# A transformer trunk's first FFN: the Winograd scheme's first step replaced by a plain one, and the modulation weights summed on TensorE

## The reference

```python
mod = silu(c) @ w_ada + b_ada                       # c (1, 1024), w_ada (1024, 9*1024)
(sh1, sc1, gt1, sh2, sc2, gt2, sh3, sc3, gt3) = split(mod, 9)
h = rms_normalize(x) * (1 + sc1) + sh1
x = x + 0.5 * gt1 * swiglu(h, w_ffn1_in, w_ffn1_out)   # swiglu: (silu(h@Wg) * (h@Wu)) @ Wout
h = rms_normalize(x) * (1 + sc2) + sh2
x = x + gt2 * hybrid_mixer(h, ...)
h = rms_normalize(x) * (1 + sc3) + sh3
x = x + 0.5 * gt3 * swiglu(h, w_ffn2_in, w_ffn2_out)
out = rms_normalize(x) * g_final
```

## Time and profile before

| | |
|---|---|
| median of 3 runs | 2015.44 us (2013.27 to 2015.57) |
| the profiled execution | 2016.27 us |
| its span, first to last instruction | 2014.5 us |
| mean granted TensorE clock | 0.977 of 2.4 GHz |
| TensorE busy | 1902.1 us (94%) |
| VectorE busy | 1170.8 us (58%) |
| ScalarE busy | 761.0 us (38%) |
| GpSimd busy | 893.9 us (44%) |

### The profile page before, as it was taken

The page is one execution under the profiler, slowest core; times in us unless marked ns, Lnnn a source line. Parts: engine busy times, 40 slices in busy tenths (PEclk is TensorE's granted clock), DMA queues, the critical chain, the costliest instruction groups (busy, mean ns, idle before and its releaser), DMA issues. The chain is left out here.

```text
span 2014.5 us, 25363 instructions
## 1 busy us (share of the span) xinstructions
PE 1902.1 (94%) x9280; PEld 1556.5 (77%) x9280; DVE 1170.8 (58%) x1680; ACT 761.0 (38%) x1390; POOL 893.9 (44%) x642
## 2 busy tenths in 40 slices
PE   4699999999999969999999999998999999999997
PEld 3488888888888857777778887777788888888886
DVE  5967666754778770544434465559434444448777
ACT  5533222322444441444431554344323323334444
POOL 4887778766000052100012133478878778710002
PEclk8799999999999979999999999999999999999999
DMA  7155656552876301311112112433223323159652
GB/s 292 53 184 171 203 174 211 184 160 84 322 274 195 114 23 42 127 43 43 43 33 74 57 42 84 154 118 104 95 94 116 105 86 124 63 207 342 208 189 84
DMA packets 208107, 267.93 MB, mean 133 GB/s; under 512 B 14303, under 2 KB 125171, under 8 KB 206451
## 3 DMA queue, kind: packets, MB, share of 16 engines
q1 hardware_dynamic: 207986, 266.34, 39.4%
HBM read 211.16 MB, written 53.03 MB: 131 GB/s over the span
## 5 line engine op out<-in xcount | busy, mean ns | idle before, releaser
L420 POOL TENSOR_TENSOR ffn_ring_b<-ffn_raw_in,ffn_ring_b 128x512 fp32r<-128x512 f32 x174 | 247.0, 1425 | 145.3 <-ACT ffn_ring_b L415 145.3
L832 PE MATMUL bank<-ffn_w_hi,ffn_a_hi 128*128 128x512 f32 x616 | 240.1, 390 | 1.2 <-DVE ffn_w_lo L816 1.2
L834 PE MATMUL bank<-ffn_w_hi,ffn_a_lo 128*128 128x512 f32 x616 | 239.7, 389 | 0.0
L833 PE MATMUL bank<-ffn_w_lo,ffn_a_hi 128*128 128x512 f32 x616 | 239.7, 389 | 0.0
L1539 POOL TENSOR_TENSOR mx_w_lo<-mx_raw_w,mx_w_hi 128x1024 fp32r<-128x1024 f32 x28 | 67.4, 2419 | 364.7 <-ACT mx_w_hi L1363 297.8
L415 ACT CAST ffn_ring_b<-ffn_raw_in 128x512 fp32r<-128x512 f32 x174 | 107.9, 621 | 299.5 <-PE bank L1267 283.9
L108 POOL TENSOR_SCALAR rms<-rms 128x1 f32<-128x1 f32 x24 | 15.1, 628 | 444.1 <-ACT ffn_junk L102 430.5
L805 ACT CAST ffn_a_hi<-ffn_a_stage 128x512 fp32r<-128x512 f32 x154 | 95.6, 621 | 203.2 <-PE bank L834 198.8
L1086 DVE TENSOR_TENSOR ffn_u<-bank,ffn_u 128x512 f32<-128x512 f32 x111 | 76.4, 688 | 163.8 <-PE bank L1267 163.4
L1265 PE MATMUL bank<-h_hi,ffn_ring_a_hi 128*128 128x512 f32 x356 | 143.0, 402 | 26.0 <-ACT ffn_g L1014 17.9
L816 DVE TENSOR_TENSOR ffn_a_lo<-ffn_a_stage,ffn_a_hi 128x512 fp32r<-128x512 f32 x154 | 106.4, 691 | 74.8 <-ACT ffn_a_hi L805 74.7
(11 more groups left out here) (336 smaller groups left out, 4673.0 us busy)
## 6 DMA issues: line engine op xcount, KB each, us to landing
ffn_raw_in<-in_w_ffn_in SPq DMA_DIRECT2D x88, 512.0 KB, 5.9
ffn_a_stage<-hidden SPq DMA_DIRECT2D x154, 256.0 KB, 3.4
ffn_w_stage<-in_w_ffn_out SPq DMA_DIRECT2D x132, 256.0 KB, 3.2
ada_rest<-in_w_ada SPq DMA_DIRECT2D x64, 448.0 KB, 4.0
hidden<-ffn_u SPq DMA_DIRECT2D x88, 256.0 KB, 2.0
hidden<-ffn_g SPq DMA_DIRECT2D x66, 256.0 KB, 2.0
mx_raw_w<-in_w_mix_in SPq DMA_DIRECT2D x28, 512.0 KB, 3.8
ada_ring<-in_w_ada SPq DMA_DIRECT2D x8, 1024.0 KB, 12.2
```

What stands on the lines that cost most here:

```text
L420: pool.tensor_tensor(self.lo(q), self.source(b, m), self.hi(q).bitcast(F32), ALU.subtract)\
L832: pe.matmul(dst, a_hi, w_hi, start=first, stop=False, skip_group_check=True)
L833: pe.matmul(dst, a_hi, w_lo, start=False, stop=False, skip_group_check=True)
L834: mm = pe.matmul(dst, a_lo, w_hi, start=False, stop=True, skip_group_check=True)
```

## The change

1. **Plain first step** (`PlainStep`, `InWeights(plain=True)`). Step 0 of the first FFN computes its 2x2 by 2x2 block product directly, 8 block products for gate and 8 for up, with no sums of weights or inputs: half 0 is the first 512 rows (b11, b21; banks 0 to 3), half 1 the last 512 (b12, b22; banks 4 to 7). Group k of 8 channel blocks takes 12 matmuls (4 output blocks x 3). All 8 weight operands have slots of their own (7 of the ring and `extra`), their low parts are made by VectorE. Steps 1 to 10 stay as they were; the Winograd operands are made beside half 1, the low parts of t3 and b22 by GpSimd in step 1, those of t1, t2, t4 by VectorE from the end of step 0 into step 1. a12 of step 0 takes another slot.
2. **TensorE sums the pieces.** For each piece k it multiplies the 16 blocks of 128 columns by the column silu(c) of k, adding in banks 1 and 2. `lead_acc` and VectorE's sums are gone. The ring has 6 slots.
3. **Order of loads.** x tiles 0 to 3 each ahead of pieces 0 to 3, pieces 4 to 7, the first weights, x tiles 4 to 7, the weights of step 1.
4. **Tiles 4 to 7** are squared and scaled between ScalarE's casts, turned between TensorE's groups of half 0, and both halves copied by VectorE (`keep_both`).

The diff, cut to its core (left out are the index changes that step 0's 8 products bring, `before(b)`, `b - FIRST`, and the same functions under new names, `square`, `scale`, `keep_high`, `keep_low`, `turn`):

```diff
     G, U, ADA, SMALL, S_TEMP = 172, 180, 188, 199, 203.125
-    ADA_RING, LEAD_ACC, START_JUNK, START_XN = 32, 140, 148, 156
+    ADA_RING, START_JUNK, START_XN = 32, 203.125, 188
     OPS, A_STAGE, W_STAGE = (140, 156), 96, 64
     T_LOW, T_HIGH = 192, 172
     TMP, XN_A, GATE, SHIFT = 122.25, 126.25, 130.25, 134.25
...
@@ -512,17 +536,23 @@
             .then_inc(self.small_loaded, 16)
         sp.dma_start(self.brow[0:self.M * KD, :], self.b_ada.rearrange("a (r n) -> (a r) n", n=P))\
             .then_inc(self.small_loaded, 16)
-        for k in range(KD):
+        def piece(k):
             if k >= self.RING:
                 sp.wait_ge(self.summed, k - self.RING + 1)
             sp.dma_start(self.ring[k % self.RING], self.w_ada[0, k * P:(k + 1) * P, 0:2 * D])\
                 .then_inc(self.ring_loaded[k % self.RING], 16)
-            if k < self.RING:
-                for t in (2 * k, 2 * k + 1):
-                    sp.dma_start(self.c.xres[:, t, :], self.x[0, t * P:(t + 1) * P, :])\
-                        .then_inc(self.x_loaded[t], 16)
-            if k == KD - 2:
-                first_weights()
+
+        def tile(t):
+            sp.dma_start(self.c.xres[:, t, :], self.x[0, t * P:(t + 1) * P, :]).then_inc(self.x_loaded[t], 16)
+
+        for k in range(4):
+            tile(k)
+            piece(k)
+        for k in range(4, KD):
+            piece(k)
+        first_weights()
+        for t in range(4, self.c.NS):
+            tile(t)
 
...
+    def pe_lead(self, pe):
         c, KD = self.c, self.c.KD
         pe.wait_ge(self.consts, 3)
         pe.wait_ge(self.small_loaded, 32)
         pe.transpose(c.bank[:, 0, 0:(self.M + 1) * KD], self.brow[:, :],
                      c.ident[0:(self.M + 1) * KD, 0:(self.M + 1) * KD]).then_inc(self.b_turned, 1)
-        for t in range(c.NS):
-            pe.wait_ge(self.xn_done, t + 1)
-            if t >= 2:
-                pe.wait_ge(self.kept_low, t - 1)
-                pe.wait_ge(self.kept_high, t - 1)
+        pe.wait_ge(self.c_act_done, 1)
+        for k in range(KD):
+            pe.wait_ge(self.ring_loaded[k % self.RING], 16 * (k // self.RING + 1))
             for half in range(2):
-                for k in range(4):
-                    mm = pe.transpose(c.bank[:, 4 + 2 * (t % 2) + half, k * P:(k + 1) * P],
-                                      self.xn[t % 2][:, (4 * half + k) * P:(4 * half + k + 1) * P], c.ident[:, :])
-                mm.then_inc(self.turned, 1)
-        for half in range(2):
-            pe.wait_ge(self.summed, KD + half)
-            for v in range(2):
-                for k in range(half * KD // 2, (half + 1) * KD // 2):
-                    r = v * KD + k
-                    mm = pe.matmul(c.bank[:, 1 + half, r:r + 1], self.acc[:, r * P:(r + 1) * P], self.ones[:, :],
-                                   start=True, stop=True)
-            mm.then_inc(self.cols_ready, 1)
...
+    def dve_lead(self, dve, weights):
         c, KD, D = self.c, self.c.KD, self.c.D
         dve.wait_ge(self.c_act_done, 1)
         dve.wait_ge(self.b_turned, 1)
         dve.tensor_copy(self.bcol[:, :], c.bank[:, 0, 0:self.M * KD]).then_inc(self.b_kept, 1)
-        tiles_after = {1: (0,), 2: (1,), 3: (2, 3), 4: (4, 5), 5: (6,), 6: (7,)}
...
+        for t in range(4):
+            self.keep_low(dve, t)
+        for m in range(8):
+            weights.cut_lo(dve, 0, m)
         dve.wait_ge(self.b_kept, 1)
...
+
+
+
+
+    def __init__(self, core, halved, weights, start, part):
+        self.c, self.hv, self.weights, self.start, self.part = core, halved, weights, start, part
+        self.ready, self.silu_done = core.sem("plain_ready"), core.sem("plain_silu_done")
+
+    def op(self, k, half):
+        return (("b11", "b12"), ("b21", "b22"))[k // 4][half]
+
+    def cut_hi(self, act, op, k, ready):
+        act.wait_ge(ready, k + 1)
+        act.copy(self.hv.hi(op, k), self.hv.source(op, k)).then_inc(self.hv.hi_done[op], 1)
+
+    def scalar(self, act, p_ready, g11_done, silu_g, at):
+        st, w = self.start, self.weights
+        C11, S1, U2, U3 = at
+        for m in range(8):
+            if m == 7:
+                act.wait_ge(st.summed, 5)
+            w.cut_hi(act, 0, m)
+        b11 = lambda k: self.cut_hi(act, "b11", k, st.h_b11)
+        b21 = lambda k: self.cut_hi(act, "b21", k, st.h_b21)
+        b11(0)
+        st.square(act, 4)
+        b11(1)
+        st.scale(act, 4)
+        st.square(act, 5)
+        b11(2)
+        st.scale(act, 5)
+        st.square(act, 6)
+        b11(3)
...
+        b21(2)
+        b21(3)
+        for half, op, made in ((0, "b12", st.h_b12), (1, "b22", st.h_b22)):
+            for k in range(4):
+                st.act_modulate(act, half, k)
+                self.cut_hi(act, op, k, made)
+        act.wait_ge(self.ready, 1)
+        act.activation(silu_g(C11), self.c.bank[:, 0, :], ACT.Silu).then_inc(g11_done, 1)
+        act.wait_ge(self.ready, 3)
+        act.activation(silu_g(S1), self.c.bank[:, 2, :], ACT.Silu).then_inc(self.silu_done, 1)
+        for m in range(3):
+            w.cut_hi(act, 1, m, p_ready)
+        self.hv.cut_hi(act, "t2")
+        act.wait_ge(p_ready, 8)
+        for bank, i in ((4, U2), (6, U3)):
+            act.activation(silu_g(i), self.c.bank[:, bank, :], ACT.Silu).then_inc(self.silu_done, 1)
+        for m in range(3, w.R):
+            w.cut_hi(act, 1, m, p_ready)
+
+    def vector(self, dve):
+
+        st, hv, w = self.start, self.hv, self.weights
+        mod = lambda k: st.dve_modulate(dve, k // 4, k % 4)
+        lo = lambda k: hv.cut_lo(dve, self.op(k, 0), ks=(k % 4,))
+        st.dve_cols(dve, 0)
+        mod(0)
+        mod(1)
+        lo(0)
+        st.dve_cols(dve, 1)
+        mod(2)
+        lo(1)
+        mod(3)
+        lo(2)
+        mod(4)
+        lo(3)
+        st.keep_both(dve, 4)
+        mod(5)
+        lo(4)
+        st.keep_both(dve, 5)
+        mod(6)
+        lo(5)
+        mod(7)
+        lo(6)
+        st.keep_both(dve, 6)
+        lo(7)
+        st.keep_both(dve, 7)
+        for k in range(4):
+            hv.cut_plain_lo(dve, "b12", k)
+            hv.make_t1(dve, st.h_b12, (k,))
+        for k in range(4):
+            hv.cut_plain_lo(dve, "b22", k)
+            hv.make_t2(dve, st.h_b22, (k,))
+
+    def hidden(self, dve, bank, i, dst, silu_done, n, ready, m, done):
+        dve.wait_ge(silu_done, n)
+        dve.wait_ge(ready, m)
+        dve.tensor_tensor(dst, self.c.bank[:, bank, :], self.part(0, i), ALU.mult).then_inc(done, 1)
+
+    def tensor(self, pe, p_ready):
+        c, hv, w, st = self.c, self.hv, self.weights, self.start
+        for half in range(2):
+            for k in range(8):
+                op = self.op(k, half)
+                if half == 0:
+                    if k == 0:
+                        pe.wait_ge(st.b_kept, 1)
+                        pe.wait_ge(st.cols_kept, 2)
+                    if k % 4 == 0:
+                        pe.wait_ge(w.lo_done, k + 4)
+                    pe.wait_ge(hv.lo_done[op], k % 4 + 1)
+                else:
+                    if k == 0:
+                        pe.wait_ge(st.kept_low, c.NS)
+                        pe.wait_ge(st.kept_high, c.NS)
+                    pe.wait_ge(hv.plain_lo_done[op], k % 4 + 1)
+                h_hi = hv.hi(op, k % 4)
+                h_lo = hv.plain_lo(op, k % 4) if half else hv.lo(op, k % 4)
+                for i in range(4):
+                    if half == 0 and k == 0 and i == 2:
+                        pe.wait_ge(st.cols_kept, 4)
+                    q = 4 * (k // 4) + i
+                    cols = slice(k % 4 * P, (k % 4 + 1) * P)
+                    w_hi, w_lo, dst = w.hi(q)[:, cols], w.lo(q)[:, cols], c.bank[:, 4 * half + i, :]
+                    pe.matmul(dst, w_hi, h_hi, start=(k == 0), stop=False, skip_group_check=True)
+                    pe.matmul(dst, w_hi, h_lo, start=False, stop=False, skip_group_check=True)
+                    mm = pe.matmul(dst, w_lo, h_hi, start=False, stop=(k == 7), skip_group_check=True)
+                    if half == 0 and k == 7:
+                        mm.then_inc(self.ready, 1)
+                    if half == 1 and k in (3, 7):
+                        mm.then_inc(p_ready, 1)
+                if half == 0 and k in (1, 2, 4, 5):
+                    st.turn(pe, {1: 4, 2: 5, 4: 6, 5: 7}[k])
...
                 for a in operands:
                     sp.wait_ge(made[a], b + 1)
-                    sp.dma_start(spill[fo_operands.index(a) * STEPS + b, :, :], place[a]).then_inc(spilled[a], 16)
+                    sp.dma_start(spill[fo_operands.index(a) * STEPS + b, :, :], place_of(b, a)).then_inc(spilled[a], 16)
 
             if start:
                 start.load(sp, lambda: weights.load(sp, 0))
-                sp.wait_ge(start.cols_ready, 2)
+                weights.load(sp, 1)
+                sp.wait_ge(start.turned, 2 * NS)
             if lead:
                 lead.sync(sp)
-            weights.load(sp, 1)
```

(74 more changed lines are left out.)

283 lines of the change are left out of this document (150 added, 133 removed).

## The result

The changed kernel takes **2024.86 us** (median of 6 runs, 2023.01 to 2026.56), the kernel before in the same rounds 2015.51: a ratio of 1.0046, 95% interval 1.0035 to 1.0057. It is 0.46% slower, 9.35 us by the medians; the forecast was 2029, in a range of 2012 to 2036. The profiled execution has a span of 2023.2 us where it was 2014.5, so the traces differ by 8.7 us.

The account below looks back on a forecast made before the run. The prediction took TensorE, busy 94% of the span, to bound the kernel. Step 1's later start and two gaps, 6.6 + 3.1 + 4.0 = 13.7 us, on 2016.3 gave 2030.0, or 2029 us by the median, range 2012 to 2036.

Parts of the forecast that it names:

- the clock column: Sign in the profile: granted clock 0.50 through the pieces if right, 1.00 before 70 us if wrong.
- Lead: Summing of the eight pieces on TensorE before step 0's products, at the low clock: first plain product at 71.9 us.
- 8.1 + 8 x 6.99 + 4 x 1.97: Sum for the lead: first piece landed at 8.1 us, eight pieces of 6.99, four tile turns of 1.97.
- Plain step: Step 0: 43.6 us of matmuls, 2.6 lost at the low clock, 4.3 of tile turns; ends at 122.4 us.
- Wait for s4: Step 1's fourth product: TensorE idles 3.1 us for ScalarE's copy, which waits for VectorE's sum s4.
- Wait before p5: Step 1: GpSimd's late ninth weight (p5), overlapping VectorE's late c22 for p3; 4.0 us taken, between 1.8 and 5.7.
- the second branch, c22: Step 1, p3: VectorE's c22 ready about 155.9 us, TensorE there at 152.8 without GpSimd's delay.
- I put nothing on step 2: Step 2: no delay charged, since GpSimd's load of 28 to 37 us for each 38 lets it catch up.
- Without these gaps step 1 costs as before: Step 1: apart from the idle gaps of 3.1 and 4.0 us, no change in its time.
- the start of step 1: End of step 0: step 1 begins at 122.4 us against 115.8 before, 6.6 us later.
- the clock rises in the lead: Rival: dense one-column products raise the clock, step 1 starts 16.7 us earlier than before, 1999 us; chance 0.14.
- In part: Rival: transposes between pieces raise the clock for a third of the lead, about 10 us less, 2019 us; chance 0.08.

Follow-up runs that it names:

- e12_b22_vec: The changed kernel with the four low parts of b22 made by VectorE, behind its sum s4, instead of GpSimd: 2024.92 us, ratio 1.0047.
- e15_no_low: The changed kernel without b22's four low parts on any engine, p3 reading the high part twice (other values): 2023.8 us, ratio 1.0041.
- e4_warm: The changed kernel with 48 transposes of the identity into an unused bank before the first piece: 2024.32 us in one execution.
- e3_row: The changed kernel with the sum's operands swapped: silu(c) stationary, 512 columns of a piece moving, the row turned to columns afterwards: 2003.58 us, ratio 0.9947.
- e5_wide: The changed kernel with 64 equal moving columns in place of one in each of the 128 summing products: 2003.23 us, ratio 0.9941.

## Why the prediction was right, and where its sizes were off

The direction held, by its own mechanism: one-column products run at 1.2 GHz through the whole lead. The pace shows it; the clock column, which the prediction named as the sign, reads 1.00 there (see the last section). Term by term:

- **Lead: 71.9 forecast, 68.85 measured.** The step that mis-sized it is "8.1 + 8 x 6.99 + 4 x 1.97". It adds durations, and each group's last record overlaps the next group by 0.2 us; start to start a piece is 6.76 and a turn 1.74. 8 x 0.23 + 4 x 0.23 = 2.8 of the 3.05, the rest is piece 0 at 7.85.
- **Plain step: 50.5 forecast, 49.7 measured** (68.85 to 118.58), with no wait in either half, as argued. The difference is again the turns of tiles, added with their durations. Step 1 starts 2.8 us late, not 6.6.
- **Wait for s4: 3.1 forecast, 1.4 measured** (1.6 by the starts, less 0.2 that the kernel before loses one product earlier). Place and releaser are those named. VectorE's chain s1 to s4 ended at 127.41 instead of 133.1: its first b12 came at 94.03 instead of 97.9, four t4 took 5.7 us instead of 6.6, and the chain itself 5.9 instead of 6.7.
- **Wait before p5: 4.0 forecast, 5.0 measured.** 3.3 us by the starts (3.17 in the row) is idle for GpSimd's low part, as named. 1.7 us is the clock at 0.50 behind it (the next 12 matmuls take 4.46 us instead of 2.72), which the forecast had not charged. e12_b22_vec and e15_no_low show that the second branch, c22, lay right behind.
- **"I put nothing on step 2": 1.2 us measured.** VectorE's work of step 1 reaches into step 2: at 169.47 ScalarE's copy has waited for VectorE's sum (L1305), and TensorE waits for the copy. 2.8 + 1.4 + 5.0 + 1.2 = 10.4, the shift of the marker.
- **"Without these gaps step 1 costs as before"** held: 118.58 to 163.36 is 44.8 us, less the gaps of 6.6 it is 38.2. What the sum left out is the work behind, which gives 1.7 us back, mostly in the mixer. The mixer's first products are slow until the clock rises, and it rises sooner after their start than before (granted 0.79 in 765 to 770 us, where the matching stretch before, 755 to 760, has 0.62). That is 1.0 us by the first long product; the other 0.7 was not traced. All of it lies within the spread named above, so it is not shown to be an effect of the change.

10.4 - 1.7 = 8.7, against the forecast's 13.7. So 3.8 us too much on the start of step 1, 1.7 on s4 and 1.7 behind the marker stand against 1.0 and 1.2 too little on the waits of p5 and step 2; that the total came as close as 5 us is in part these terms cancelling. The rivals: "the clock rises in the lead" is refuted by the lead's pace and by e4_warm; e3_row and e5_wide show what it would have been worth: with the clock up for most of the lead the plain step starts 20 to 22 us earlier and the time is 2003 us, where the rival had 28 us and 1999. "In part" is refuted too: all pieces of the changed kernel run at one pace, and in e4_warm a clock that was up at piece 0 was gone at piece 1. The best versions are those with VectorE's sum, 1999.4 to 2001.1 us, which can't be told apart.

## What to carry to other kernels

Price TensorE work that is long and thin at the low clock unless a trace shows that form at the high one; being busy is not enough, and a wider moving operand can be cheaper than a narrow one. Add start-to-start times, not durations. Before moving operations from one to the other of two full engines, look whether the second is full in the same stretch and slows the first; a wait that has a second one right behind it gives nothing back when it is removed. Charge a wait with the slow products that follow it as well, where the clock falls.

## What the runs showed of the hardware that was not expected

- A raised clock fell with TensorE busy for 2.00 of 2.00 us, between one-column products (e4_warm, 16 us).
- The same 32 records take 6.83 us with one moving column and 6.93 with 64 at 1.2 GHz, 3.63 and 3.68 at 2.4 GHz. 512 float32 columns take 0.44 us a record at the high clock (7.03 for 16).
- The granted-clock column reads 1.00 in the lead of the changed kernel, in every stretch of 10 us, while the pace is that of 1.2 GHz throughout. In e4_warm, where the clock rose first, the column follows its fall. In this case, then, ahead of the first recorded change the pace is to be read, as was done with the earlier trace rows.
- The same low part, 128 x 512, takes 0.62 us on VectorE alone (2.48 for four, at 117.68 us in the changed kernel, with GpSimd idle) and 1.44 with GpSimd at the same kind of work (5.77 for four, e12_b22_vec). The Trainium skill ("GPSIMD Engine Reference", section 1, Specifications) has the two share their interfaces to SBUF, with contention when VectorE reads two inputs from it; the trace agrees, and GpSimd pays as well (6.30 against 5.06 for four).
- A wait of 3.2 us was enough to bring the clock down in the middle of step 1 (granted 0.50 from 147 to 149 us), and so was one of 2.0 us in e4_warm (0.50 from 146 to 148), while waits of 1.2 to 1.4 us left it up.
